# Row-tiled score products in the first pass of the first attention

## The reference, cut to what matters

```python
qa = rope(qa.reshape(b, s, A_HEADS, HEAD_DIM), pos)      # A_HEADS = 12, HEAD_DIM = 64
ka = rope(ka.reshape(b, s, A_HEADS, HEAD_DIM), pos)
# each group g: queries and keys split by residue class mod dilation, then a causal window of 128 keys
s = jnp.einsum('nbqd,nbkd->nbqk', qb, kb) * (dh ** -0.5)
s = jnp.where(mask[None], s, -jnp.inf)
lse = jax.nn.logsumexp(s, axis=-1)
p = jnp.exp(s - lse[..., None])
# head slot j of the three groups is then mixed by softmax over their lse
```

## Time and profile before

| | |
|---|---|
| median of 3 runs | 3112.95 us (3112.75 to 3118.0) |
| the profiled execution's own time | 3124.41 us |
| its span in the profile | 3121.2 us |
| TensorE matmul busy | 2987.4 us, 96% |
| TensorE weight load busy | 2315.2 us, 74% |
| VectorE busy | 1492.0 us, 48% |
| ScalarE, GpSimd busy | 948.7 us, 770 us |
| granted TensorE clock, mean | 0.972 |

### The profile page before, as it was taken

How to read it: one execution, slowest core, us unless ns; L and a number is a source line. 1 busy time by engine, 2 the same in 40 slices (tenths; PEclk the granted TensorE clock), 3 DMA queues, 4 the chain that set the end, 5 groups by cost and what they waited for, 6 DMA issues and landing times.

```text
span 3121.2 us, 37530 instructions
## 1 busy us (share of the span) xinstructions
PE 2987.4 (96%) x13944; PEld 2315.2 (74%) x13944; DVE 1492.0 (48%) x1743; ACT 948.7 (30%) x1524; POOL 769.8 (25%) x502
## 2 busy tenths in 40 slices
PE   6999999999999999999999999999999999899998
PEld 5887875556677777778888888877777777677766
DVE  6454564554433435364343444333264454466654
ACT  4323235665300012331122211122134234244441
POOL 4302112222233321123333333322201101300025
PEclk9999999999999999999999999999999999798999
DMA  6101000000211110011111111112100001000023
GB/s 224 53 15 34 28 21 14 9 20 19 81 49 44 47 38 26 29 34 47 47 47 47 47 47 47 47 41 81 36 15 14 22 1 36 6 6 6 1 103 120
DMA packets 166350, 128.72 MB, mean 41 GB/s; under 512 B 19264, under 2 KB 150048, under 8 KB 165968
## 3 DMA queue, kind: packets, MB, share of 16 engines
q1 hardware_dynamic: 164816, 118.55, 12.5%
q10 hardware_dynamic: 1408, 8.50, 0.7%
HBM read 114.20 MB, written 12.65 MB: 41 GB/s over the span
## 4 chain that ended last, share of the span: by engine, by line
PE 65%; DVE 5%; issue 2%; ACT 2%; DMA 1%; SPq 0%; POOL 0%; DVEq 0%; ACTq 0%; POOLq 0%
PE ps L705 17%; PE ps L707 16%; PE ps L706 16%; PE ps L2745 4%; PE ps L2584 3%; PE ps L618 2%; PE ps L2835 1%; PE ps L2837 1%; PE ps L2836 1%; PE ps L2643 1%; PE ps L2644 1%; PE ps L2645 1%; PE ps L644 0%; DVE probs_low L2185 0%; PE ps L701 0%
## 5 line engine op out<-in xcount | busy, mean ns | idle before, releaser
L705 PE MATMUL ps<-NH,w_high 128*128 128x512 f32 (+1 forms) x1992 | 779.9, 392 | 21.1 <-POOL w_low L1016 6.7
L706 PE MATMUL ps<-NL,w_high 128*128 128x512 f32 (+1 forms) x1992 | 781.2, 392 | 0.0
L707 PE MATMUL ps<-NH,w_low 128*128 128x512 f32 (+1 forms) x1992 | 778.5, 391 | 0.0
L1014 POOL CAST w_high<-w_raw 128x1024 fp32r<-128x1024 f32 x193 | 208.4, 1080 | 2169.7 <-PE ps L707 1191.0
L1016 POOL TENSOR_TENSOR w_low<-w_raw,w_high 128x1024 fp32r<-128x1024 f32 x193 | 480.9, 2492 | 15.4
L705 PEld LDWEIGHTS ps<-NH,w_high 128*128 128x128 f32 x1992 | 379.4, 190 | 115.3 <-issue 19.9
L706 PEld LDWEIGHTS ps<-NL,w_high 128*128 128x128 f32 x1992 | 378.9, 190 | 83.5
L707 PEld LDWEIGHTS ps<-NH,w_low 128*128 128x128 f32 x1992 | 379.3, 190 | 82.7
L769 DVE TENSOR_TENSOR hT<-hT,ps 128x1024 f32<-128x1024 f32 x168 | 205.1, 1221 | 250.2 <-PE ps L707 250.2
L705 PE MATMUL ps<-act_high,w_high 128*128 128x512 f32 x352 | 141.4, 402 | 2.9 <-DVE act_low L1886 2.9
L707 PE MATMUL ps<-act_high,w_low 128*128 128x512 f32 x352 | 139.4, 396 | 0.0
(11 more groups left out here) (400 smaller groups left out, 5335.9 us busy)
## 6 DMA issues: line engine op xcount, KB each, us to landing
w_raw<-in_w_in SPq DMA_DIRECT2D x69, 512.0 KB, 3.8
w_raw<-in_w_up SPq DMA_DIRECT2D x44, 512.0 KB, 3.8
w_raw<-in_w_out SPq DMA_DIRECT2D x24, 512.0 KB, 3.3
w_raw<-in_w_down SPq DMA_DIRECT2D x22, 512.0 KB, 3.8
w_raw<-in_w_xkv SPq DMA_DIRECT2D x8, 512.0 KB, 5.9
x_in<-in_x SPq DMA_DIRECT2D x8, 512.0 KB, 9.2
residual_spill<-hT SPq DMA_DIRECT2D x1, 4096.0 KB, 13.5
hT<-residual_spill ACTq DMA_DIRECT2D x1, 4096.0 KB, 13.0
```

The lines of the kernel that those rows point to most:

```text
L705: nc.tensor.matmul(o, wh, xh, start=start, stop=False)
L706: nc.tensor.matmul(o, wh, xl, start=False, stop=False)
L707: return nc.tensor.matmul(o, wl, xh, start=False, stop=stop)
L1014: nc.gpsimd.tensor_copy(WH[slot][:, :], w_raw[slot][:, :]).then_inc(w_high, 1)
```

## The change

In the first pass the score products contract only the 64 partitions of their head, in all three groups. Groups 0 and 1 go together: tile t of group 0 and tile t of group 1 are issued behind each other, then their two masks. For this group 1 holds its heads the other way round (`a_half`): when group 0 uses partitions 0 to 63, group 1 uses 64 to 127. The weight tiles of group 1's queries and keys are therefore loaded in two DMAs, one for each half of the columns, and the second waits for the first (`load_turned`, by `load_parts`). `a_order` lets units of groups 0 and 1 take turns, and TensorE waits for two banks at once. The second pass still contracts all 128 partitions.

```diff
@@ -108,6 +108,15 @@
 V_BF = V_KVN + 1
 V_END = V_BF + 1
 
+TURNED = 4
+
+
+def a_half(g, h):
+
+    h = 1 - h if g == 1 else h
+    return slice(HD * h, HD * h + HD)
+
+
 def a_order():
 
 
@@ -116,7 +125,7 @@
     out, unit = [], 0
     banks = [(g, u) for g in range(A_GROUPS) for u in range(4 if g < 2 else 2)]
     for h in range(2):
-        for x, (g, u) in enumerate(banks):
+        for x, (g, u) in enumerate([(g, u) for u in range(4) for g in range(2)] + banks[8:]):
             out.append(("p1", h, g, u, unit))
             unit += 1
             if (h, x) == (0, 3):
@@ -778,7 +787,7 @@
             sp.nop(nofuse=True)
             for dst, src in parts[:-1]:
                 sp.dma_start(dst(w_raw[slot]), src).then_inc(w_part, 16)
-            sp.wait_ge(w_part, (before + len(parts) - 1) * 16)
+            sp.wait_ge(w_part, (TURNED + before + len(parts) - 1) * 16)
             sp.nop(nofuse=True)
             dst, src = parts[-1]
             sp.dma_start(dst(w_raw[slot]), src).then_inc(w_landed[slot], 16)
@@ -797,6 +806,12 @@
                 kc = src.shape[1]
                 sp.dma_start(w_raw[slot][:, first:first + kc * n].rearrange("p (c n) -> p c n", c=kc),
                              src).then_inc(w_landed[slot], 16 // len(parts))
+
+        def load_turned(sp, st, i, w, before, src, col):
+
+            half = lambda t, x: t.rearrange("p (c n) -> p c n", c=C)[:, :, HD * x:HD * x + HD]
+            load_parts(sp, st, i, w, before, [
+                (lambda t: half(t, 0), src[:, :, col + HD:col + P]), (lambda t: half(t, 1), src[:, :, col:col + HD])])
 
         w_in = a["w_in"].rearrange("l (c p) n -> (l p) c n", p=P)
         w_xkv = a["w_xkv"].rearrange("l (c p) n -> (l p) c n", p=P)
@@ -862,7 +877,10 @@
                 for g in range(A_GROUPS):
                     for n, first in enumerate((QA, KA, VA)):
                         col = first + g * 256 + p * P
-                        load_tile(sp, A, 0, 3 * g + n, (0, P, w_in[:, :, col:col + P]))
+                        if g == 1 and n < 2:
+                            load_turned(sp, A, 0, 3 * g + n, 2 * p + n - TURNED, w_in, col)
+                        else:
+                            load_tile(sp, A, 0, 3 * g + n, (0, P, w_in[:, :, col:col + P]))
                         if (p, g, n) == (0, 0, 2):
 
                             for k in range(2, 2 + NT):
@@ -1591,7 +1609,7 @@
             dve.wait_ge(spilled, 16)
             for g in range(A_GROUPS):
                 for h in range(2):
-                    link(nc.vector.memset(qA[g][h][HD * (1 - h):HD * (1 - h) + HD, :], 0.0))
+                    link(nc.vector.memset(qA[g][h][a_half(g, 1 - h), :], 0.0))
             dve.wait_ge(rope_in, 32)
 
             def rope(A, p, k, dst, g):
@@ -1666,7 +1684,7 @@
                 link(r)
                 nc.vector.sem_inc(job_free[A.slot(k)], 1)
 
-            q_dst = lambda g: [(qA[g][h], slice(HD * h, HD * h + HD)) for h in range(2)]
+            q_dst = lambda g: [(qA[g][h], a_half(g, h)) for h in range(2)]
             k_dst = lambda g: [(kA[g], slice(0, P))]
             for p in range(2):
                 A = st_a[p]
@@ -2336,22 +2354,31 @@
                 for what in a_order():
                     if what[0] == "p1":
                         _, h, g, u, unit = what
-                        pe.wait_ge(a_q, 6 * p + 2 * g + 2)
-                        wait_bank(pe, A, 0, unit)
-                        b = bank[A.bank(unit)]
+                        if g == 1:
+                            continue
+                        both = range(2) if g == 0 else (2,)
+                        pe.wait_ge(a_q, 6 * p + 2 * both[-1] + 2)
+                        for y in range(len(both)):
+                            wait_bank(pe, A, 0, unit + y)
                         per = 4 if g == 2 else 2
                         for x in range(per):
-                            t = per * u + x
-                            q_ = qA[g][h][:, t * P:(t + 1) * P]
-                            if g == 2:
-                                o, ks, mk = b[:, x * P:(x + 1) * P], t * P, m_pair
-                            elif t % (NT // A_DIL[g]) == 0:
-                                o, ks, mk = b[:, x * 256 + P:x * 256 + 256], t * P, m_own
-                            else:
-                                o, ks, mk = b[:, x * 256:x * 256 + 256], (t - 1) * P, m_band
-                            nc.tensor.matmul(o, q_, kA[g][:, ks:(t + 1) * P], start=True, stop=False)
-                            mm = nc.tensor.matmul(o, identb, mk, start=False, stop=True)
-                        mm.then_inc(unit_done, 1)
+                            t, to = per * u + x, []
+                            for g_ in both:
+                                b = bank[A.bank(unit + (g_ == 1))]
+                                if g_ == 2:
+                                    o, ks, mk = b[:, x * P:(x + 1) * P], t * P, m_pair
+                                elif t % (NT // A_DIL[g_]) == 0:
+                                    o, ks, mk = b[:, x * 256 + P:x * 256 + 256], t * P, m_own
+                                else:
+                                    o, ks, mk = b[:, x * 256:x * 256 + 256], (t - 1) * P, m_band
+                                rows = a_half(g_, h)
+                                nc.tensor.matmul(o, qA[g_][h][rows, t * P:(t + 1) * P], kA[g_][rows, ks:(t + 1) * P],
+                                                 start=True, stop=False)
+                                to.append((o, mk))
+                            for y, (o, mk) in enumerate(to):
+                                mm = nc.tensor.matmul(o, identb, mk, start=False, stop=True)
+                                if x == per - 1:
+                                    mm.then_inc(unit_done, 1)
                     elif what[0] == "vt2":
                         turn_values(2)
                     elif what[0] == "mt":
```

## The result

| | before | after |
|---|---|---|
| median | 3115.17 us (4 runs) | 3146.44 us (4 runs, 3142.74 to 3150.17) |
| ratio, 95% interval | | 1.0089 [1.0068, 1.0109] |
| profiled execution, its span | 3124.41, 3121.2 us | 3142.74, 3140.9 us |
| mean granted clock | 0.972 | 0.964 |
| p1's first product to p2's first, p = 0 / p = 1 | 24.95 / 24.88 us | 37.30 / 37.20 us |

The change makes the kernel 0.9% slower: +31 us by the medians, 21 to 34 by the interval. The forecast was +8.2, its range ended at +17. The stage itself, from the first score product to p2's first, grew by 12.35 and 12.32 us, 24.7 in all, and this lies inside the interval. What is beyond it differs between executions.

A forecast was written before the change was run, and what follows sets the result against it. TensorE, busy 96% of the span, was taken as the bound. Per pass, head 0 +2.55, head 1 +0.55 and the end +0.98 made 4.1; two passes +8.2, from 3112.95 to 3121.2 us, range 3108 to 3130.

The forecast's parts named there:

- rival C: p1's pairs: switches cost, but all passes of a pair overlap; 2.1 us per pass, +4.2, 3117.2 us; chance 0.13.
- Part 1: p1, 64-row products between 128-row masks: each round trip costs 0.32 us (bounds 0 and 0.41), 16 per head.
- Part 2: p1's pairs on opposite halves: queue order lets only part of their passes overlap; pairs cost +0.55 us per head.
- Rival E: p1: half the array idle could bring the 1.2 GHz clock; +38 us, 3151; chance 0.04.
- The end of p1: Head 1's group 2 and fillers beside VectorE's row chain: TensorE finishes last, barely; +0.98 us per pass.
- rival F: p1: 64-row products run as full ones; only the row chain's later place counts, +0.8 us per pass, 3114.6; chance 0.06.
- VectorE's maxima: VectorE in p1: as many as before, 0.69 us per unit, about 1.4 per pair against TensorE's 2.1; cost nothing.
- rival D: p1: 64-row halves need no drain and run side by side; -7.6 us, 3105.4, or 3108.2 with half the overlap; chance 0.12.
- The split loads: Group 1's weight tiles, loaded in two DMAs: at most 7.6 us in all, covered by earlier work, so cost nothing.

The follow-up runs named there:

- m1_fill: Kernel before, 11 fillers ahead of p2 replaced by 96 bf16 products: 64 rows (p = 0), 64 and 128 in turns (p = 1); 0.216 and 0.32 us apart.
- x4_samehalf: Changed kernel with group 1's heads on the same half of the rows as group 0's, no turned loads; 3164.41 us, ratio 1.0145 to the kernel before.
- m2_fill: Kernel before, fillers replaced: 96 over 128 rows (p = 0), 192 on opposite halves in turns (p = 1); at full clock 11 and 22 products in 2 us.
- x7_batch64: Changed kernel with all score products of a bank (two banks in groups 0 and 1) ahead of their masks; 3112.08 us, ratio 0.9976 to the kernel before.
- x8_g2batch: Kernel before with only group 2 over 64 rows, a unit's four products ahead of its four masks; 3121.81 us, ratio 1.0003.
- x1_order: Changed kernel with its order, turned halves and split loads, but every score product over all 128 rows; 3119.7 us, ratio 0.9996 to the kernel before.
- x2_g2full: Changed kernel with group 2's products over all 128 rows again, groups 0 and 1 still in pairs; 3123.33 us, ratio 1.0011 to the kernel before.
- run 22: Not a label of a run: "run" is the verb, for 22 bf16 products on opposite halves in 2 us, measured in m2_fill.
- x3_g2only: Kernel before with only group 2's products over their head's 64 rows: no pairs, order change or split loads; 3134.29 us, ratio 1.0047.
- x5_batch: Changed kernel with score products batched ahead of their masks and group 2 over all 128 rows; 3119.96 us, ratio 1.0 to the kernel before.
- x6_batchfull: Kernel before with each unit's masks behind all its score products, everything over 128 rows; 3118.47 us, ratio 0.9996.

## Why the prediction was wrong

The direction held, the size and its main cause did not. What the forecast counted was too small to carry the direction: with the overlap as it turned out, its own sum is rival C's +4.2 us, less than the 6.2 that it took to be told from no change. That the kernel is clearly slower is the clock's doing, so the direction was partly luck.

- **Part 1, the round trip**: right. A tile of group 2 took 0.58 us, as forecast. m1_fill gives 0.105 per switch with products that are otherwise back to back. The rest of the 0.32 stands between the two passes of a product: in the tile at 181.37 they start 0.21 us apart, though 128 columns take 0.107, and the second weight load starts only 0.11 behind the first. The trace agrees with TensorEngine Tiling (Array Packing) of the Trainium skill, Key Properties: a change of the tiling mode drains the engine; for 64 rows it is now shown.
- **Part 2, the overlap**: the first step that failed is "group 1's first pass can start only when group 0's second does". It made the forecast too high by 2 us per pass. The pair of 256 spans 0.63 us, with 0.11 between its passes and 0.10 ahead of the masks, so its four passes take 0.43, rival C's case. x4_samehalf (1.06 in place of 0.63) and m2_fill (22 against 11 in 2 us) show it by itself. The queue of the kernel before could not speak for this: it held no two products that use different rows. Head 0 grew by 1.52 us, close to rival C's 1.57, in place of 2.55. TensorE: Matmul & The Clock Gate of the Trainium skill, Part 3, has tiles on different rows run side by side; it was weighed at 0.13 against the order of the queue, and the trace agrees with it.
- **Rival E, the clock**: the step that failed and made the size. The sum put the clock at nothing. It was given 0.04 with "the clock stays at 1.00 throughout p1, and drains are 0.1 us long". The first holds for a p1 without drains and says nothing about one with them; and the trace of the kernel before held a fall under a busy TensorE elsewhere, at 1162.4 us (line 618). The second counted a drain by its length and not by how often it returns: the forecast itself had a group 2 tile take 0.58 us for 0.27 of passes, eight times in a row. At full clock the stage would have grown by some 2.1 us, an estimate by rival C's sum, which head 0 bears out; it grew by 12.3, so about 10 per pass, 20 of the 25 us, is the clock. Rival E's size was of the right order (+38 for all of p1), but its cause, half the array idle, is wrong: x7_batch64, x8_g2batch and m1_fill's p = 0 keep half of it idle at 1.00.
- **The end of p1**: the row behind the last unit of group 0 costs 0.8 us where TensorE is quick enough, as rival F had it (0.75 and 0.81 in x1_order and x2_g2full). In the change itself it cost nothing, since TensorE was the slower one.
- **VectorE's maxima**, put at nothing outside rival D: they cost 0.38 us per pass in the change and 0.58 to 0.59 at full clock, since a pair asks for two banks at once.
- **The split loads**: right, they cost nothing. x1_order has them and shows no loss, and GpSimd splits tile 3 after the same 2.04 us, at 93.34, with the later start.
- **Rival D** had a saving in it that is real (the overlap), but not without the drain. With fewer drains it comes: x7_batch64 gains 0.24% [0.08, 0.4].

Shown: which edit takes the clock down, that batching keeps it up, and that neither 64 rows nor long products with switches lower it alone. Not needed for a fall: a switch (line 618 in the kernel before). Open: what in a run of short products and switches it is.

## What to carry to other kernels

Use opposite halves of the rows in long runs: issue all half-row products of a bank or two behind each other, and the full-row ones behind them, since each change costs 0.1 us and the fp32 product behind it another 0.1 between its passes. A product without a partner for the other half gained nothing from 64 rows here (x8_g2batch). When an edit puts short gaps into TensorE's stream, or makes its products very short, price the clock too, for all that follows: it can fall although TensorE never waits, and what stands behind the stretch pays. And where an edit makes TensorE arrive earlier at a wait, look at the clock behind the wait and try longer fillers: here they saved 1.6 us per pass.

## What the runs showed of the hardware

- Four fp32 passes of two products on opposite halves of the rows take the time of two (0.43 us), and bf16 products run 22 in 2 us in place of 11.
- The granted clock fell to its lower level with TensorE busy without a wait: behind eight tiles of 64-row fp32 products and full masks in turns (4.61 us), inside 80 short bf16 products that changed their rows each time, and, in the kernel before, inside 48 fp32 products of 2 columns that changed nothing (at 1162.4 us). In the change, half-row pairs with masks in turns did not bring it back in the 13 us that followed, while full-row tiles did so in x3_g2only. TensorE: Matmul & The Clock Gate of the Trainium skill, Part 1, tells of a kernel with frequent micro-idles between groups of matmuls whose clock went up and down. In this case's traces it fell behind such a stretch as well (at 185.7 in the change); that the short gaps did it is not shown.
- A wait of 2.02 us behind fillers was followed by the lower clock (x5_batch), waits of 1.71 (x2_g2full), 1.47 (x7_batch64) and 1.22 (x6_batchfull) were not.
